# Spreading dependent chains over more weight units in a two-layer transformer kernel: convolution, gates, decays, the recurrence's norm, and the masked copies of its levels

## The reference, cut to what matters

```python
h = rmsnorm(x, norm_mix_g)
c_g, b_g, xa, za, q, fl, iv, og, ga, gb = split(h @ w_in)
ya = b_g * causal_dwconv3(c_g * xa, conv_w) * silu(za)
log_f = logaddexp(log(max(lb, 1e-30)), log1p(-lb) + log_sigmoid(fl))
kk = (1 - lb) * sigmoid(-fl)
o = hgrn2(silu(q), kk, iv, log_f)      # 8 heads of 128, gated linear recurrence
o = o * rsqrt(mean(o * o) + eps) * hg_norm_g
yb = o * silu(og)
m = sigmoid(ga) * (ya @ w_a) + sigmoid(gb) * (yb @ w_b)
x = x + m @ w_o
x = x + sigmoid(rmsnorm(x) @ w_ple_gate) * (p @ w_ple_proj)
out = rmsnorm(x)
```

## Time and profile before

| what | us |
|---|---|
| median of 3 runs (2838.80 to 2840.16) | 2839.46 |
| the profiled execution's own time | 2839.11 |
| its span, first to last instruction | 2837.3 |
| PE busy | 2791.3 (98%) |
| DVE busy | 1819.0 (64%) |
| ACT busy | 1408.7 (50%) |
| POOL busy | 678.7 (24%) |

### The profile page before, as it was taken

One profiled execution on the slowest core, in us unless ns is written; L12 is line 12 of the kernel. 1 busy time (PEld: TensorE's weight loads), 2 busy tenths in 40 slices (PEclk: granted clock), 3 DMA queues, 4 the chain that ended last, 5 costly groups with the idle time before them and its releaser, 6 DMA issues.

```text
span 2837.3 us, 39091 instructions
## 1 busy us (share of the span) xinstructions
PE 2791.3 (98%) x14972; PEld 2401.0 (85%) x14972; DVE 1819.0 (64%) x2904; ACT 1408.7 (50%) x1990; POOL 678.7 (24%) x365
## 2 busy tenths in 40 slices
PE   8999999999999999999999999999999999999998
PEld 6888888888888888888888888888888889999886
DVE  5566766877777755555555555666777866555555
ACT  5454654455555544444444444546745545444454
POOL 0000000388888888700000000001201111000000
PEclk9999999999999999999999999999999999999999
DMA  7653478777777777767677777666554546666564
GB/s 260 206 161 119 135 245 322 238 189 192 187 192 188 191 188 190 192 214 225 209 223 223 213 236 234 223 206 184 172 181 148 157 147 190 187 187 191 186 195 154
DMA packets 199018, 559.02 MB, mean 197 GB/s; under 512 B 53344, under 2 KB 69872, under 8 KB 195888
## 3 DMA queue, kind: packets, MB, share of 16 engines
q1 hardware_dynamic: 161456, 554.99, 62.9%
q0 software_dynamic: 36944, 0.41, 2.7%
q10 hardware_dynamic: 432, 1.12, 0.1%
HBM read 535.32 MB, written 21.12 MB: 196 GB/s over the span
## 4 chain that ended last, share of the span: by engine, by line
PE 89%; DVE 4%; ACT 3%; issue 2%; DMA 2%; POOL 0%; DVEq 0%; ACTq 0%; SPq 0%
PE bank L528 88%; DVE wlo L904 2%; ACT whi L1606 2%; PE bank L540 1%; DMA raw<-in_w_dv 1%; DVE QKb L907 0%; DVE tmpc L907 0%; DMA h_scratch<-X 0%; DMA raw<-in_w_pq 0%; ACT L1606 0%; ACT DD L1606 0%; POOL tmpc L1586 0%; DMA raw<-in_w_dk 0%; DVE DD L907 0%; ACT EB L1606 0%
## 5 line engine op out<-in xcount | busy, mean ns | idle before, releaser
L904 DVE TENSOR_TENSOR wlo<-raw,whi 128x1024 fp32r<-128x1024 f32 (+1 forms) x965 | 1188.2, 1233 | 849.3 <-ACT whi L1606 847.2
L1606 ACT ACTIVATE whi<-raw 128x1024 fp32r<-128x1024 f32 (+1 forms) x965 | 1016.2, 1056 | 1000.1 <-PE bank L528 980.6
L528 PE MATMUL bank<-aX,whi 128*128 128x512 f32 (+1 forms) x4000 | 968.9, 392 | 0.4 <-ACT whi L1606 0.3
L528 PE MATMUL bank<-whi,aX 128*128 128x512 f32 x3008 | 934.8, 391 | 11.3 <-ACT whi L1606 8.7
L528 PEld LDWEIGHTS bank<-aX,whi 128*128 128x128 f32 (+1 forms) x4000 | 729.5, 188 | 142.8 <-issue 4.2
L528 PEld LDWEIGHTS bank<-whi,aX 128*128 128x128 f32 x3008 | 565.8, 188 | 131.0 <-ACT whi L1606 9.1
L1566 POOL DMA_INDIRECT gate_scratch<-gate,place x256 | 577.0, 2254 | 262.1 <-DMA gate_scratch<-HB 184.0
L528 PE MATMUL bank<-wlo,aX 128*128 128x512 f32 x1504 | 587.5, 391 | 3.5 <-DVE wlo L904 3.4
L528 PE MATMUL bank<-aX,wlo 128*128 128x256 f32 (+1 forms) x3984 | 531.3, 284 | 9.6 <-DVE wlo L904 7.9
L528 PEld LDWEIGHTS bank<-aX,wlo 128*128 128x128 f32 (+1 forms) x3984 | 513.5, 191 | 31.1 <-DVE wlo L904 8.9
L528 PEld LDWEIGHTS bank<-wlo,aX 128*128 128x128 f32 x1504 | 282.8, 188 | 65.2 <-DVE wlo L904 7.5
(11 more groups left out here) (227 smaller groups left out, 1814.8 us busy)
## 6 DMA issues: line engine op xcount, KB each, us to landing
raw<-in_w_down SPq DMA_DIRECT2D x256, 512.0 KB, 3.7
raw<-in_w_up SPq DMA_DIRECT2D x256, 512.0 KB, 4.3
raw<-in_w_in SPq DMA_DIRECT2D x176, 512.0 KB, 4.0
raw<-in_w_out SPq DMA_DIRECT2D x32, 512.0 KB, 4.1
gate_scratch<-HB SPq DMA_DIRECT2D x16, 1024.0 KB, 7.6
raw<-in_w_pq SPq DMA_DIRECT2D x32, 512.0 KB, 5.6
raw<-in_w_o SPq DMA_DIRECT2D x32, 512.0 KB, 3.8
raw<-in_w_pg SPq DMA_DIRECT2D x32, 512.0 KB, 4.1
```

The costliest lines, as they stand in the source:

```text
L528: return e.matmul(o, lhsT, rhs, start=start, stop=stop, skip_group_check=True)
L904: e.tensor_tensor(wlo[:, s, 0:n], raw[:, r, 0:n], whi[:, s, 0:n].bitcast(F32), ALU.subtract).then_inc(s_lo, 1)
L1606: return e.activation(o, i, f, **k)
```

## The change

The arithmetic is the same and so is PE's work; operations move to later or earlier units, each by one or a few places, and one activation of a single column is added.

- `weight` runs one tile ahead from tile 119 on to 122.
- The turns of kp 0 to 3, and their `high_two` and `low_two`, come one unit later.
- In `decay` each link of the chain gets a step of its own on ACT, and DVE's operations follow (k up to 26 for 22). 
- The masked copies of a level stand at 1, 3 and 5 (two there) of its 7 units, instead of at 0, 1, 2, 3.
- The recurrence's norm: the reciprocal at k = 69 instead of 67, the products at 70 and 71 instead of 68 and 69, the turns at 74 to 77 instead of 72 to 75. The square root on ACT stays at 67.
- The convolution: `T1*T0` and the taps come one group later (after `bg`), `T3*T2` one later (after `za`), Silu and gate after the next round's `cg`, high and low part after the next `xa`. Those of round 7 stand in `ga` 0 and `gb` 0.
- ACT computes a Sigmoid of one column just after the square root ahead of `pg`.

```diff
@@ -379,6 +379,8 @@
     Q20, OG0 = G["q2", 0].first + 1, G["og", 0].first
+    DECAY = dict(zip((0, 1, 6, 7, 8, 9, 10, 11, 12, 13, 14, 15, 17, 20, 21, 22, 23, 24, 25, 26),
+                     (0, 1, 4, 5, 6, 7, 8, 9, 10, 11, 12, 13, 14, 15, 16, 17, 18, 19, 20, 21)))
     RESCALED = ([("fl", i) for i in range(8)] + [("q2", i) for i in range(8)] + [("og", i) for i in range(8)]
@@ -643,8 +645,8 @@
                 last.then_inc(s_hv, 1)
-            if 72 <= k < 76:
-                hp = k - 72
+            if 74 <= k < 78:
+                hp = k - 74
                 w.wait_ge(s_hr, 5)
@@ -666,8 +668,8 @@
                 row_of(R3F, 2, ones, diag)
-            if UP1 - 7 <= u < UP1 - 3:
-                end_turn(u - UP1 + 7)
+            if UP1 - 6 <= u < UP1 - 2:
+                end_turn(u - UP1 + 6)
             if u in (UP1, UP1 + 1):
@@ -676,7 +678,7 @@
                 scores((u - PQ0) // 8 - 1)
-            if OG0 <= u < OG0 + 76:
+            if OG0 <= u < OG0 + 78:
                 hgrn(u - OG0)
@@ -1146,8 +1148,8 @@
                 e.memset(AT[:, :, :], 0.0).then_inc(s_at, 1)
-            if 0 <= k < 56 and k % 7 < 4:
-                n, s = k // 7 - 1, k % 7
+            for s in {1: (0,), 3: (1,), 5: (2, 3)}.get(k % 7, ()) if k < 56 else ():
+                n = k // 7 - 1
                 b, _ = HLF[n + 1][s]
@@ -1167,15 +1169,16 @@
                 e.tensor_scalar(lbs[:, 0:2, :], lbs[:, 0:2, :], 1.0 / 128, EPS, ALU.mult, ALU.add).then_inc(s_hr, 1)
+            if k == 69:
                 w.wait_ge(s_hq, 1)
                 e.reciprocal(lbs[:, 2:4, :], lbs[:, 0:2, :]).then_inc(s_hr, 1)
-            if 68 <= k < 70:
-                t = k - 68
+            if 70 <= k < 72:
+                t = k - 70
                 v = DD[:, t, :].rearrange("p (h c) -> p h c", h=8)
...
                 tt(v, v, lbs[:, 2 + t, :].unsqueeze(2).to_broadcast([128, 8, 128]), ALU.mult).then_inc(s_hr, 1)
-            if 72 <= k < 76:
-                hp = k - 72
+            if 74 <= k < 78:
+                hp = k - 74
                 b, _ = HYF[hp]
@@ -1238,9 +1241,9 @@
                 route(*ROUTE[u])
-            if Q20 <= u < Q20 + 23:
-                decay(u - Q20)
-            if OG0 <= u < OG0 + 76:
+            if u - Q20 in DECAY:
+                decay(DECAY[u - Q20])
+            if OG0 <= u < OG0 + 78:
                 hgrn(u - OG0)
@@ -1260,8 +1263,8 @@
                     tt(o, banks[b], HB[:, t * D + g * 512:t * D + g * 512 + 512], ALU.add).then_inc(s_free[b], 1)
-            if -5 <= x < -1:
-                low_two("mix", x + 5)
+            if -4 <= x < 0:
+                low_two("mix", x + 4)
             if x in (1, 2):
@@ -1429,11 +1432,12 @@
             step(UP0 + 2 * i + 1)
-            weight(i + 2)
+            weight(i + 2 + (i > 116))
+            if i == 116:
+                weight(119)
             lower_bounds(i)
...
                 tt(cols[:, C_NMX:C_NMX + 16], cols[:, C_NMX:C_NMX + 16], cols[:, C_FIN:C_FIN + 16], ALU.mult).then_inc(s_gm, 1)
-        weight(122)
         for j in range(16):
@@ -1462,11 +1466,27 @@
         T = [tmpc[:, j, :] for j in range(6)]
+
+        def conv_gate(i):
+            w.wait_ge(s_sz, i + 1)
+            w.wait_ge(s_cv, 6 * i + 5)
+            tt(T[5], T[3], T[4], ALU.mult).then_inc(s_cv, 1)
+
+        def conv_low(i):
+            w.wait_ge(s_yh, i + 1)
+            tt(yaL[:, i, :], T[5], yaH[:, i, :].bitcast(F32), ALU.subtract).then_inc(s_yl, 1)
+
         for i in range(8):
...
             whole(G["cg", i], T[0])
+            if i:
+                conv_gate(i - 1)
             steps(G["xa", i])
             whole(G["xa", i], T[1])
+            if i:
+                conv_low(i - 1)
+            steps(G["bg", i])
+            whole(G["bg", i], T[3])
             w.wait_ge(s_rw, RESCALE["xa", i])
@@ -1475,18 +1495,11 @@
             e.scalar_tensor_tensor(T[2][:, 2:256], T[1][:, 0:254], cw[:, 0, i:i + 1], T[2][:, 2:256], ALU.mult, ALU.add).then_inc(s_cv, 1)
-            steps(G["bg", i])
-            whole(G["bg", i], T[3])
+            steps(G["za", i])
+            whole(G["za", i], T[4])
             w.wait_ge(s_rw, RESCALE["bg", i])
...
             tt(T[3], T[3], T[2], ALU.mult).then_inc(s_cv, 1)
-            steps(G["za", i])
-            whole(G["za", i], T[4])
-            w.wait_ge(s_sz, i + 1)
-            w.wait_ge(s_cv, 6 * i + 5)
-            tt(T[5], T[3], T[4], ALU.mult).then_inc(s_cv, 1)
-            w.wait_ge(s_yh, i + 1)
-            tt(yaL[:, i, :], T[5], yaH[:, i, :].bitcast(F32), ALU.subtract).then_inc(s_yl, 1)
@@ -1494,6 +1507,8 @@
                     whole(G[name, i], tmpc[:, 2 * (i % 3) + j, :])
+                    if i == 0:
+                        (conv_low if j else conv_gate)(7)
                 g = G["ao", i]
@@ -1639,11 +1654,11 @@
         def finish(x):
-            if x == -6:
+            if x == -5:
                 w.wait_ge(s_gm, 1)
                 w.wait_ge(s_um, 128)
-            if -6 <= x < -2:
-                high_two("mix", x + 6)
+            if -5 <= x < -1:
+                high_two("mix", x + 5)
             if x in (1, 2):
@@ -1686,27 +1701,30 @@
         def decay(k):
-            p = 0 if k in (0, 2, 10, 14) else 1
+            p = {0: 0, 1: 0, 4: 0, 13: 0, 14: 0, 15: 0, 19: 0}.get(k, 1)
             x, t1, t2, b_, dd = decay_cols(p)
...
                 w.wait_ge(s_rw, RESCALE["fl", 7])
-            if k in (0, 1):
+            if k in (0, 2):
                 act(t1, x, ACT.Abs).then_inc(s_da, 1)
+            if k in (1, 3):
                 w.wait_ge(s_da, 2 * p + 1)
                 act(t1, t1, ACT.Exp, scale=-1.0).then_inc(s_da, 1)
-            if k in (2, 3):
+            if k in (4, 5):
                 w.wait_ge(s_da, 2 * p + 2)
                 act(t1, t1, ACT.Ln, bias=1.0).then_inc(s_da, 1)
-            if k in (10, 13):
+            if k in (13, 16):
                 w.wait_ge(s_dc, 8 + 3 * p)
                 act(t1, t1, ACT.Abs).then_inc(s_da, 1)
+            if k in (14, 17):
                 w.wait_ge(s_da, 7 + 3 * p)
                 act(t1, t1, ACT.Exp, scale=-1.0).then_inc(s_da, 1)
+            if k in (15, 18):
                 act(dd, dd, ACT.Exp).then_inc(s_da, 1)
-            if k in (14, 15):
+            if k in (19, 20):
                 w.wait_ge(s_da, 8 + 3 * p)
                 act(t1, t1, ACT.Ln, bias=1.0).then_inc(s_da, 1)
-            if k == 22:
+            if k == 26:
                 w.wait_ge(s_rw, RESCALE["q2", 7])
@@ -1779,9 +1797,9 @@
                 act(gt, gt, ACT.Exp).then_inc(s_gx, 1)
-            if Q20 <= u < Q20 + 23:
+            if Q20 <= u < Q20 + 27:
                 decay(u - Q20)
-            if OG0 <= u < OG0 + 76:
+            if OG0 <= u < OG0 + 78:
                 hgrn(u - OG0)
@@ -1918,35 +1937,47 @@
         act(og[:, :, :], og[:, :, :], ACT.Silu).then_inc(s_og, 1)
+        def conv_silu(i):
+            w.wait_ge(s_rw, RESCALE["za", i])
+            act(tmpc[:, 4, :], tmpc[:, 4, :], ACT.Silu).then_inc(s_sz, 1)
+
+        def conv_high(i):
+            w.wait_ge(s_cv, 6 * i + 6)
+            act(yaH[:, i, :], tmpc[:, 5, :], ACT.Copy).then_inc(s_yh, 1)
+
         for i in range(8):
...
             half(G["cg", i], tmpc[:, 0, :])
+            if i:
+                conv_silu(i - 1)
             steps(G["xa", i])
...
             half(G["xa", i], tmpc[:, 1, :])
+            if i:
+                conv_high(i - 1)
             steps(G["bg", i])
...
             half(G["za", i], tmpc[:, 4, :])
-            w.wait_ge(s_rw, RESCALE["za", i])
-            act(tmpc[:, 4, :], tmpc[:, 4, :], ACT.Silu).then_inc(s_sz, 1)
-            w.wait_ge(s_cv, 6 * i + 6)
-            act(yaH[:, i, :], tmpc[:, 5, :], ACT.Copy).then_inc(s_yh, 1)
         for i in range(16 + LAG):
...
                     steps(g)
-                    if i < 3:
+                    if i < 2:
+                        w.wait_ge(s_cv, 46 + 2 * i)
+                    elif i == 2:
                         w.wait_ge(s_yl, 8)
...
                     half(g, tmpc[:, 2 * (i % 3) + j, :])
+                    if i == 0:
+                        (conv_high if j else conv_silu)(7)
                 steps(G["ao", i])
@@ -1965,6 +1996,7 @@
         root()
+        act(st[:, 31:32], cols[:, 0:1], ACT.Sigmoid)
         for i in range(4):
...
             steps(g)
```

## The result

The changed kernel takes 2823.77 us in the median of six runs (2822.45 to 2824.56), the kernel before, measured beside it, 2839.81 (2837.96 to 2841.36): ratio 0.9944, with a 95% interval of 0.9931 to 0.9956. That is 16.0 us less where 19.4 were forecast, inside the range and on the side of its upper end. It is 3.8 us from the forecast of 2820, outside the 2.8 us to which 0.70 was given, and 1.7 us from the centre of the first rival. The profiled execution has a span of 2821.6 us, 15.7 under that of before.

What follows compares the result with a forecast made beforehand. PE was taken as the bound, busy 2791.3 of 2837.3 us, losing time to late operations in in-order queues; 7.9 + 5.8 + 4.3 + 1.5 + 0.4 - 0.8 + 0.3 = 19.4 us off 2839.46 gave 2820.0, within 2.8 us at 0.70.

Steps and rivals of the forecast that it cites:

- the first rival: Half the waits come back: levels keep 4 of 7.9, norm and decays 1.5 together; 2825.5 us, chance 0.13.
- Levels: Levels and convolution: six levels take 146.5 us where 138.6 would do; the whole 7.9 us is won.
- the one on the copies: Levels: copies waited 10.9 us for PE's turns; moved later they don't, and the pair, 1.5 us, just fits a unit.
- each `QKb` product 1.1 us or more before the turn that reads it: Levels: from following the queues through rounds 0 to 3, each product is done at least 1.1 us ahead.
- its signs: If right, clock 1.00 and no PE wait between 2100 and 2340; waits for `wlo` or `QKb` would mean DVE is full.
- The norm: Units 789 to 793: the late split comes in time; gain 5.8 us, less 0 to 0.4 at unit 794.
- Decays: Units 693 to 708: with a link per step ACT and DVE keep their leads; gain 4.3 us.
- End of `up`: Weights a tile ahead win 1.5 us; turns a unit later win net 0.4 after a new 0.9 wait at 673.
- `ao` 0: Unit 805: round 7's low part, behind `whole` of `gb` 0, makes PE wait anew; 0.8 us lost.
- Sigmoid: At `pg`: eviction in time wins 1.3 us, unit 932 and `pg` 1 lose 0.5 each; net 0.3.
- the rival of dearer tables: A table change stops ACT for another 1.28 us per load, delaying Silu and gate; some 4.5 less, 2824.5 us, chance 0.03.
- The new waits don't come: Rival: units 673, 805 and 932 lose nothing, 2.2 us more won; 2817.8 us, chance 0.06 for below 2817.2.

Runs made afterwards that it cites:

- the convolution alone: The kernel before with only the convolution's Silu, gate, high and low parts and taps moved as in the change: 2827.57 us, ratio 0.9956.
- the norm back: The changed kernel with the recurrence's norm, and its turns, in the steps they had before: 2823.64 us, ratio 0.9942.
- the convolution back: The changed kernel with the convolution's chain in its old order on DVE and ACT, copies still two in a unit: 2835.0 us, ratio 0.9983.
- the copies alone: The kernel before with only the masked copies moved, two of them in one unit: 2843.33 us, ratio 1.0011.
- the copies back: The changed kernel with the masked copies one in each of four steps again, each a step behind its turn: 2822.17 us, ratio 0.9937.
- the mended version: The changed kernel with its three new waits (units 673, 805, 932) taken away by moving the low parts, rounding and early Sigmoid: 2820.35 us.

## Why the prediction came out as it did

**Levels, forecast -7.9, measured -6.3.** The size of the loss, 7.9 us against the undisturbed level, was right to 0.1: the convolution alone wins it all. The step that failed is the one on the copies, "one to three units later the turn is long done. The price is two copies in one unit, 1.5 us, beside a split of 1.2 in a unit of 2.8: just full". The forecast took the old waits of 10.9 us as a cost and the pair as free. It is the other way round: beside the new chain the waits are free and the pair costs 1.6 us. Beside the old chain the exchange costs 3.1, 1.8 of it by the clock; what the waits alone cost there no run shows. The statement "each `QKb` product 1.1 us or more before the turn that reads it" failed at three units. At 743 ACT stands before POOL's product of `og` 7 (1.84 us), then does a Silu of 1.92, neither of which the forecast names, and DVE enters the stretch late. At 778 the round's taps, the pair and the product stand together on DVE, from 2266.53 to 2273.74 without a gap, and at 771 likewise. It also had splits at 1.2 us where some take 1.77, in the trace of before too (2156.77). One step was wrong in its favour: DVE's wait for the Silu doesn't stay at 1.3 us in a round, it goes from 9.1 us in seven waits to 2.4 in six, the longest 0.7 (2100 to 2345).

Of its signs, the clock is 1.00 between 2100 and 2340. But PE waits 0.9 us for `QKb` there, which was to say that DVE is full. It is, in those stretches and not in the level: it is busy for 190 of the 240 us.

**The norm, forecast -5.8 less 0 to 0.4, measured -5.2.** The number is nearly right, with the 0.4 at unit 794 as foreseen (3.20 instead of 2.80). The forecast named the five things ahead of the split, "the reduction (2.28 us), the square root, a wait for POOL, the taps and a product of 1.2", and booked the gain under the norm without saying what each is worth. The wait for POOL and the taps belong to the convolution's edit, and they are most of it: taking the norm's own edit away costs 0.7 us, and the convolution alone wins 4.5. To give the whole gain to the norm's edit, as the theory of the run with the norm back did, was wrong. The two edits overlap: the norm's place is worth 0.7 us when the taps are gone (36.49 against 35.75). With the taps there it is worth 2.1: 38.85 with the convolution back against 40.96 with the copies alone, two kernels that differ here in nothing else. At unit 792 it is 2.7, 1.1 of waiting (3.53 against 2.40) and 1.6 because the clock fell behind the longer wait and not behind the shorter; 0.6 is lost again at unit 796. Because all edits were present, the sum came out right however the gain is shared; that it did is no proof of the share.

**Decays, -4.3 and -4.3.** Right, and shown by the run without the edit.

**End of `up`, -1.9 and -1.6.** The weights won 1.4 of 1.5. The new wait at 673 was foreseen as 0.9; it is 0.81 us of idle time and 1.1 by distance. The forecast had itself said that a unit loses more than its idle time, and didn't apply it to its new waits.

**`ao` 0, +0.8 and +1.0.** The same: 0.73 of idle, 1.0 by distance.

**Sigmoid, -0.3 and +0.1.** The wait at 932 was forecast as "0.5 too late" and is 0.56, which costs 0.9. The wait of the eviction went as forecast (1.3), and the next one shows with 0.55. The activation behind the load of 1.28 us, at 2714.69, starts at 2715.98, 0.01 behind its end, and the load begins 0.02 behind the end of the operation ahead of it: the drain of some 1.38 us that the Trainium skill (ScalarE: Activation LUTs, "What ACT_TABLE_LOAD costs") adds is not in this trace either. Of this trace's 53 loads 46 stand so, with both gaps under 0.05 us, and the rival of dearer tables is out.

**The sum.** Of the 3.4 us by which 16.0 falls short of 19.4, 1.6 are the pair of copies, 0.6 the norm's part (0.4 of them foreseen) and 1.0 the new waits and the weights; the last 0.2 lie between the medians and the lengths. The rival "half the waits come back" is right in its mechanism and not in its size. Its words, "where the taps (1.8 us), the two copies and a `QKb` product fall into neighbouring units, DVE gets more than it can do", describe units 771 and 778, and without the taps unit 743. But that costs 1.6 us where the rival has 4, with the copies back none of it is left, and the decays keep nothing. "The new waits don't come" was realized only in the mended version.

## What to carry to other kernels

A wait in an in-order queue costs only if it delays something with a deadline; measure its price by the consumer's distances, not by its own length. Where several late things stand in one queue ahead of one split, the gain belongs to the queue and not to any of them: price each edit with the others undone, or say that they share it. Work gathered into one unit to save waits makes a stretch without gaps, and the place to put it is behind the product with the next deadline, or nowhere. And a stall of PE costs its length and in some executions 1 to 2 us more, where the clock falls behind it.

## What the runs showed of the hardware

**The clock.** In the earlier trace rows the granted clock fell to 0.83 behind 3.52 us of idle PE, and it did so behind 3.35 us at unit 743 with the copies alone. There it cost 1.8 us: 8.88, less 3.69 for the unit with its turn and 3.35 of waiting. It fell too behind 3.36 us with the convolution back and behind 3.53 us at unit 792 with the copies alone. But the length of the wait doesn't decide it alone. At unit 771 PE waited 1.96 us in two runs. With the copies alone the clock fell behind it (columns as in the earlier trace rows):

```profile
2260.00:2270.00 10.00, 8.04 (x40) 6.78 (x39) 8.21 (x11) 3.88 (x6) 1.30 (x2) 0.83 0.54 157
```

With the convolution back it did not, and there the turn's matmuls took 1.16 us and not 1.80 (PE in order of time, then the stretch):

```profile
2259.08 1.16 PE L530 MATMUL bank<-QKb 128*128 128x128 f32 x8 [1.96 <-DVE QKb L909]
...
2260.00:2270.00 10.00, 10.00 (x65) 8.98 (x64) 7.34 (x9) 4.22 (x5) 1.12 (x2) 1.00 0.49 158
```

The same kernel kept its clock through 2.40 us of idle PE at 2331.39. The first block has the best sample. At unit 130 PE waits 1.19, 1.40 and 0.28 us within four, the same in all 14 traces; in seven the clock falls behind that (mean 0.83 to 0.86 in 435 to 445) and the unit takes 8.4 to 8.8 us, in the other seven it stays at 1.00 and the unit takes 7.2 or 7.3. The stretch in the changed kernel and then, in the second row, with the copies back:

```profile
435.00:445.00 10.00, 7.13 (x42) 5.91 (x41) 6.26 (x15) 5.05 (x11) 0.00 (x0) 1.00 0.95 392
...
435.00:445.00 10.00, 7.18 (x31) 5.84 (x32) 4.72 (x13) 5.05 (x11) 0.00 (x0) 0.83 0.96 395
```

No single length of wait fits these rows; what they bear out is that the same short wait may cost 1 to 2 us more, or not, from one execution to the next. Why one of two equal waits brought the clock down stays open.

**DVE beside POOL.** Between 2090 and 2345 POOL's product of 128x256 took 0.73 to 0.75 us in 31 of 36 rows of before, and 1.65 in five. In the changed kernel 21 take 0.84 to 0.86, and seven take 1.64 or 1.65. All twelve of the long ones begin 0.16 or 0.17 us inside a TENSOR_TENSOR of DVE of 128x1024. Two of them, POOL in order of time:

```profile
2150.92 1.65 POOL L1601 TENSOR_TENSOR tmpc<-tmpc,rows 128x256 f32<-128x256 f32 x1 [8.91 <-DVE tmpc L909]
...
2156.46 1.65 POOL L1601 TENSOR_TENSOR tmpc<-tmpc,rows 128x256 f32<-128x256 f32 x1 [3.89 <-DVE tmpc L909]
```

DVE's products there begin at 2150.76 and 2156.31 and keep their length, but the splits behind them take 1.77 and 1.75 us instead of 1.2. It looks as if POOL waited for DVE's product and DVE's next operation for POOL. Some 0.5 us on DVE a time is a price of overlapping the two engines that the forecast didn't have, though the trace of before has it five times. It was read from these rows and not tested by a run of its own.

**Where the scatter is.** The 14 profiled executions end unit 415, in the first block and outside the change, between 1245.6 and 1248.2 us. Behind it, parts with equal code agree to 0.1, but for the copies alone at unit 771. So what the traces scatter by lies in the first block, 1.1 to 1.6 us of it at unit 130, and a comparison by unit lengths is sharper than one by totals. It is one of single executions, though. Those without a trace can't be divided so, and the clock moves them too: the slowest of 15 executions of the kernel before took 2842.8 us at a mean granted clock of 0.995, the fastest 2838.0 at 0.998. With the copies alone it is 2846.4 at 0.995 and 2840.1 at 0.998.
